# Hybrid retention, state-space and attention step: retention scores placed between two halves of the key-value products, masks ahead of the recurrence, and the last state-space outputs inside z's first unit

## The chip, the cores and the metric

One core of a Trainium2 chip runs the whole program. The metric is the device time of one execution in microseconds (us). Engine names are those of the profile: PE is TensorE, PEld its weight loads, DVE VectorE, ACT ScalarE, POOL GpSimd, SP SyncE, whose queue carries most DMAs.

## The reference, cut to what matters

Two layers of a diffusion backbone run for 128 context tokens and 512 latent tokens that share their weights: 640 token columns in 5 chunks of 128. Layer 0 mixes with retention (8 heads) and a Mamba-2 state-space recurrence (16 heads) side by side, both in both directions; layer 1 with softmax attention. Each is followed by a convolutional feed-forward block. Every recurrence is computed by chunks:

```python
def step(s, inp):
    qc, kc, vc, ac = inp
    cum = jnp.cumsum(ac, axis=1)
    ...
    scores = jnp.einsum('bigd,bjgd->bgij', qc, kc)
    y = jnp.einsum('bgij,bgrij,bjgrv->bigrv', scores, decay, vc)
    y = y + jnp.einsum('bigd,bgrdv->bigrv', qc, s) * jnp.exp(cum)[..., None]
    ...
    s = s * jnp.exp(last)[..., None] + jnp.einsum('bjgd,bjgrv,bgrj->bgrdv', kc, vc, w)
    return s, y
...
y_ret = jax.nn.silu(g) * (y_ret * gn_gain)
y_ssm = (ssm_ys[0] + ssm_ys[1]).reshape(b, L, SSM_D_INNER)
y_ssm = rms_norm(y_ssm * jax.nn.silu(z)) * norm_gain
out = jnp.concatenate([y_ret, y_ssm], axis=-1) @ w_out
...
def conv_ffn(h, w_up, conv_w, conv_b, w_down):
    u = dwconv3(h @ w_up, conv_w, conv_b)
    a, val = jnp.split(u, 2, axis=-1)
    return (jax.nn.silu(a) * val) @ w_down
```

## The kernel before, in words

Every engine has its own program, written out by hand, and semaphores tie them. No scheduler decides an order: what a function issues is what the engine runs, in that order.

**Dense stages.** A stage is a product of the 640 columns with a weight matrix, in units of 128 output features. SP loads a unit's weights into one of 4 buffers `raw`, ACT splits off a high part (`act_split`, L360), DVE the rest (`low_split`, L368), each into one of 2 buffers. PE (`pe_tile`, L379) makes for each k-tile of 128 inputs three products of the parts (high x high, low x high, high x low), in two halves of 320 columns: 6 matmuls a tile, and 8 or 7 tiles a unit. The accumulator of unit f lies in PSUM banks 0 and 1 or 2 and 3 by turns (`pj`), and must have been read (`pj_read`) before unit f + 2 begins. So unit r + 2 needs its `w_lo`, which needs PE to be done with unit r, and the reading of unit r.

**State-space part** (`pe_ssd`, `act_ssd`, `dve_ssd`, `pool_ssd`). 16 heads in 8 pairs. For pair p PE makes five decay products (`pe_decay` 0 to 4, L1250 to L1257), after the second of them the states from the keys and the weighted inputs `xw` (`pe_states`, L1281), later the products of the states with the queries (`pe_inter`, L1294). POOL makes `xw` for both directions (L1424) for pair p once the states of pair p - 2 are there. ACT turns each decay product into `E` (`act_decay`, L1268), fills `Tx` with the skip term (`act_skip`, L1340), copies the final state out (L1358) and reads the outputs (L1363). DVE runs the recurrence `Sst` (L1394, L1401), weighs `E` by the scores (L1384, L1386), scales the state outputs into `inter` (L1406) and adds them to `Tx` (L1414). The outputs of pair p (`pe_out`, L1305 and L1308, 5 chunks in two groups) need both, and PE issues them inside pair p + 1. After the last pair a ninth pass issues the outputs of pair 7 alone. Then follows stage z (`pe_z`), whose unit 0 uses banks 2 and 3, whose unit 1 needs a `w_lo` that ACT and DVE make only after ACT has read the outputs of pair 7.

**Retention** (`pe_ret`, `act_ret`, `dve_ret`). 8 heads in 4 pairs; the two heads of a pair lie in partitions 0 to 63 and 64 to 127. For pair p PE makes the scores (`pe_ret_scores`, L1611), for each chunk head 0 and head 1 in turn, into the PSUM regions `R` that also hold the outputs of pair p - 1, so it waits until ACT has copied them (`ret_yc`, L1709). DVE masks them into `PTr` (L1763). The key-value products (`pe_ret_states`, L1625, 16 calls) feed the recurrence on DVE (`recur`, L1753, six steps `ret_rec`). The outputs (`pe_ret_out`, L1644 and L1655) go through chunks 0 to 4, and wait after chunk 0 for all six steps. ACT and DVE then normalise (L1769, L1776, L1717, L1725), PE transposes (`pe_ret_turn`, L1634), DVE and ACT gate and split for stage wo_ret (`pe_wo_ret`).

**Down projections.** `pe_first` (L407) begins a stage while its input is still being made: it runs the tiles of unit 0 as they come, and inserts two tiles of unit 1 before the last tile of unit 0. In layer 0, DVE also computes parts of the modulation (`dve_late`, L563 to L576) between the steps of these stages. The stages are dn00 (8 tiles a unit), dn01 and dn02 (7 tiles).

## Time and profile before

| | |
|---|---|
| median of 3 runs | 1973.29 us (1973.1 to 1974.2) |
| the profiled execution | 1970.14 us, of which 1968.4 us from its first to its last instruction |
| PE busy | 1896.4 us, 96% of the span |
| DVE, ACT, POOL busy | 64%, 42%, 6% |
| end of the state-space part, start of z | about 258 to 266 us |
| retention pairs | about 560 to 610 us |
| starts of dn00, dn01, dn02 | about 795, 954 and 1102 us |

In a timeline, each row gives the start, the time from the start of the first instruction merged into it to the end of the last, the engine, line, operation and names, the count and, in brackets, how long the engine sat idle before it and what released it. The matmuls of PE overlap: the step from one row's start to the next start tells more than a duration. One f32 product of the program shows as two instructions of L1611, L1625, L1634, L1644, L1655 or L1281. The buffers `E` of even pairs lie in `u_sb` and `t_sb`, `Tx` lies in `hf`, `qd` in `t_sb`.

### The profile page before, as it was taken

The numbers are of one execution on the slowest core, as the hardware profiler recorded it, in microseconds if no ns is written. First come the engines' busy times: TensorE is split into PE (matmuls) and PEld (weight loads), VectorE is DVE, ScalarE is ACT, GpSimd is POOL, SyncE is SP. The second block draws the span as 40 slices with busy tenths as digits, with TensorE's granted clock in tenths as the row PEclk, the third lists the DMA queues.
The fourth block names the chain that finished last, engine by engine and source line by source line (L and its number), as shares of the span: only waits on it lengthen the run. The fifth ranks groups of instructions, "written<-read, shape, count | busy, mean of one in ns | idle before, by whom it ended". The sixth has DMA issues, their size and how long they took to land.

```text
span 1968.4 us, 33247 instructions
## 1 busy us (share of the span) xinstructions
PE 1896.4 (96%) x13415; PEld 1800.2 (91%) x13415; DVE 1267.4 (64%) x2101; ACT 817.2 (42%) x1367; POOL 122.5 (6%) x106
## 2 busy tenths in 40 slices
PE   7999999999999999999999999899999999999999
PEld 4998789999988899999999989866698999999999
DVE  5555944666877877878978876656536553553553
ACT  4645732222435355234234344555525541441441
POOL 0011200000010000000000025411100000000000
PEclk9999999999999999999999999999999999999999
DMA  8221012444321323443433322100012222222222
GB/s 308 86 77 34 17 49 89 140 147 151 102 81 54 129 100 119 144 128 115 152 128 115 110 89 68 57 1 1 1 54 61 74 69 80 76 71 76 75 69 79
DMA packets 57065, 175.96 MB, mean 89 GB/s; under 512 B 7552, under 2 KB 9472, under 8 KB 56832
## 3 DMA queue, kind: packets, MB, share of 16 engines
q1 hardware_dynamic: 55152, 172.17, 27.1%
q10 hardware_dynamic: 1808, 2.36, 0.3%
q8 instruction: 69, 1.13, 0.2%
q14 instruction: 36, 0.29, 0.0%
HBM read 170.05 MB, written 4.46 MB: 89 GB/s over the span
## 4 chain that ended last, share of the span: by engine, by line
PE 84%; DVE 9%; ACT 4%; issue 2%; DMA 1%; SPq 1%; POOL 0%; ACTq 0%; DVEq 0%
PE ps L379 70%; PE ps L2103 2%; PE ps L2088 2%; DVE t_sb L772 1%; DVE h_lo L782 1%; PE ps L879 1%; DVE w_lo L368 1%; PE ps L2056 1%; DVE PT L2220 1%; PE ps L1294 1%; PE ps L2055 1%; ACT w_hi L360 1%; PE ps L1281 1%; PE ps L1305 1%; DMA x<-in_x 1%
## 5 line engine op out<-in xcount | busy, mean ns | idle before, releaser
L379 PE MATMUL ps<-h_hi,w_hi 128*128 128x320 f32 x2768 | 637.5, 311 | 7.8 <-DVE w_lo L368 2.9
L379 PE MATMUL ps<-h_lo,w_hi 128*128 128x320 f32 x2768 | 633.0, 310 | 9.0 <-DVE h_lo L782 7.8
L379 PE MATMUL ps<-h_hi,w_lo 128*128 128x320 f32 x2768 | 629.8, 308 | 0.0
L368 DVE TENSOR_TENSOR w_lo<-raw,w_hi 128x1024 fp32r<-128x1024 f32 (+1 forms) x218 | 267.2, 1226 | 452.6 <-ACT w_hi L360 452.3
L360 ACT ACTIVATE w_hi<-raw 128x1024 fp32r<-128x1024 f32 (+1 forms) x221 | 230.6, 1043 | 695.4 <-PE ps L379 695.2
L379 PEld LDWEIGHTS ps<-h_lo,w_hi 128*128 128x128 f32 x2768 | 461.4, 188 | 16.1 <-DVE h_lo L782 14.5
L379 PEld LDWEIGHTS ps<-h_hi,w_hi 128*128 128x128 f32 x2768 | 460.5, 188 | 15.1 <-issue 5.2
L379 PEld LDWEIGHTS ps<-h_hi,w_lo 128*128 128x128 f32 x2768 | 462.6, 188 | 0.0
L379 PE MATMUL ps<-hid_hi,w_hi 128*128 128x320 f32 x704 | 160.9, 309 | 4.4 <-DVE hid_lo L981 2.5
L379 PE MATMUL ps<-hid_hi,w_lo 128*128 128x320 f32 x704 | 160.2, 308 | 0.0
L379 PE MATMUL ps<-hid_lo,w_hi 128*128 128x320 f32 x704 | 160.2, 308 | 0.0
L379 PEld LDWEIGHTS ps<-hid_hi,w_hi 128*128 128x128 f32 x704 | 117.3, 188 | 6.1 <-DVE hid_lo L981 3.8
L379 PEld LDWEIGHTS ps<-hid_lo,w_hi 128*128 128x128 f32 x704 | 117.7, 188 | 0.0
L379 PEld LDWEIGHTS ps<-hid_hi,w_lo 128*128 128x128 f32 x704 | 117.6, 188 | 0.0
L566 DVE SCALAR_TENSOR_TENSOR maccB<-mrawB,csil,maccB 128x512 f32<-128x512 f32 x168 | 115.2, 744 | 0.0
L894 DVE SCALAR_TENSOR_TENSOR x<-ps,modT,x 128x128 f32<-128x128 f32 (+2 forms) x216 | 81.2, 431 | 14.0 <-PE ps L379 14.0
L2075 DVE TENSOR_REDUCE nmax<-ps 128x1 f32<-128x640 f32 (+1 forms) x80 | 57.0, 714 | 39.4 <-PE ps L2056 39.3
L965 ACT ACTIVATE hid_hi<-hf 128x640 f32 (+1 forms) x44 | 32.5, 739 | 112.2 <-DVE hf L979 112.2
L845 ACT ACTIVATE t_sb<-ps,fconv 128x640 f32<-128x640 f32 x88 | 77.3, 879 | 0.0
L862 DVE SCALAR_TENSOR_TENSOR t_sb<-u_sb,fconv,t_sb 128x635 f32<-128x635 f32 x88 | 76.9, 874 | 0.0
L859 DVE SCALAR_TENSOR_TENSOR t_sb<-u_sb,fconv,t_sb 128x635 f32<-128x635 f32 x88 | 76.9, 873 | 0.0
L844 ACT ACTIVATE u_sb<-ps 128x640 f32<-128x640 f32 x104 | 71.4, 687 | 2.2 <-PE ps L379 2.2
(285 smaller groups left out, 2014.7 us busy)
## 6 DMA issues: line engine op xcount, KB each, us to landing
raw<-in_ffn_up SPq DMA_DIRECT2D x88, 512.0 KB, 3.6
raw<-in_hyb_in SPq DMA_DIRECT2D x49, 512.0 KB, 3.8
mrawB<-in_w_modB SPq DMA_DIRECT2D x48, 512.0 KB, 4.2
mrawA<-in_w_modB SPq DMA_DIRECT2D x64, 256.0 KB, 2.8
raw<-in_ffn_down SPq DMA_DIRECT2D x32, 448.0 KB, 3.3
raw<-in_hyb_out SPq DMA_DIRECT2D x16, 512.0 KB, 4.2
raw<-in_ffn_down SPq DMA_DIRECT2D x16, 512.0 KB, 3.6
modw<-in_w_modA SPq DMA_DIRECT2D x12, 512.0 KB, 13.3
```

The source lines that it names most:

```text
L360: act.activation(w_hi[:, i % 2, 0:n], raw[:, b % RAW, 0:n], ACT.Copy).then_inc(S("w_hi"), 1)
L368: eng.tensor_tensor(w_lo[:, i % 2, 0:n], raw[:, b % RAW, 0:n], w_hi[:, i % 2, 0:n].bitcast(F32), SUB).then_inc(S("w_lo"), 1)
L379: last = pe.matmul(pj(f)[:, hh, :], w[:, i % 2, k * 128:(k + 1) * 128], v[:, k, hh * HALF:(hh + 1) * HALF], start=(k == 0 and n == 0), sto ...
L566: ins = dve.scalar_tensor_tensor(acc, w, c, acc, MUL, ADD)
L844: act.activation(two(u_sb[:, r % 2, :]), pj(s.f0 + r), ACT.Copy).then_inc(S("cv_u"), 1)
L845: act.activation(two(t_sb[:, r % 2, :]), pj(s.f0 + r), ACT.Identity, bias=cw[:, r + 4 * j, 3:4] if isinstance(j, int) else cw[:, ds(r + 4 ...
L859: dve.scalar_tensor_tensor(t[:, :, 1:128], u[:, :, 0:127], w(0), t[:, :, 1:128], MUL, ADD).then_inc(S("cv_mid"), 1)
L862: dve.scalar_tensor_tensor(t[:, :, 0:127], u[:, :, 1:128], w(2), t[:, :, 0:127], MUL, ADD).then_inc(S("cv_done"), 1)
L894: ins = dve.scalar_tensor_tensor(xs_, out[:, hh, a0:a1], gate(r, g), xs_, MUL, ADD)
L2075: dve.tensor_reduce(nmax[:, n % 4:n % 4 + 1], score(n), AX.X, MAX, negate=True).then_inc(S("at_m"), 1)
L2088: last = pe.transpose(TP[:, b, :], Pr[n % 3][:, b * 128:(b + 1) * 128], ident)
L2103: last = pe.matmul((B6, B7)[u % 2][64 * par:64 * par + 64, 0:256].rearrange("p (m t) -> p m t", m=2), v, PT[:, u % 2, b - b0, par:AR:2, :] ...
```

## The change

Five edits, each in the program of one or two engines:

1. `pe_z`: PE issues five tiles of z's unit 0 before the outputs of pair 7, and three after. The ninth pass issues nothing on PE.
2. `act_ssd`: the skip term is made after the copy of the final state, no longer after the second decay. `pool_ssd`: of the forward direction, the product for the last chunk, which nobody reads, is left out (4 chunks in place of 5).
3. Retention on PE: of the key-value products of the next pair the first 8 calls, then the scores of head 0 (as soon as its outputs are copied), those of head 1, then the other 8 calls. Retention on DVE: the two masks come ahead of the recurrence.
4. `pe_ret_out`: chunks in the order 0, 2, 3, 1, 4; chunks 2 and 3 wait for four steps of the recurrence, 1 and 4 for six.
5. `pe_first`: in dn00, dn01 and dn02 four tiles of unit 1 come before the last tile of unit 0, in place of two.

```diff
@@ pe_first
-                steps = [(0, k) for k in range(K - 1)] + [(1, 0), (1, 1), (0, K - 1)] + [(1, k) for k in range(2, K)]
+                m = 4 if units[0][0].name[:3] == "dn0" else 2
+                steps = [(0, k) for k in range(K - 1)] + [(1, k) for k in range(m)] + [(0, K - 1)] + [(1, k) for k in range(m, K)]
@@ pe_ssd
-                if p:
+                if 0 < p < PAIRS:
                     pe_out(pe, p - 1, (0, 1, 2))
...
-                if p:
+                if 0 < p < PAIRS:
                     pe_out(pe, p - 1, (3, 4))
@@ act_ssd
                         act_decay(act, p, i)
-                        if i == 1:
-                            act_skip(act, p)
...
                                    ACT.Copy).then_inc(S("ssd_so"), 1)
+                    act_skip(act, p)
                     act_decay(act, p, 3)
@@ pool_ssd
                 for d in range(2):
-                    scaled(xw[:, p % 2, d, :, :], wdt[:, :, d, 2 * p:2 * p + 2].unsqueeze(3).to_broadcast([128, NCH, 2, 64]))
+                    n = NCH - 1 + d
+                    scaled(xw[:, p % 2, d, 0:n, :], wdt[:, 0:n, d, 2 * p:2 * p + 2].unsqueeze(3).to_broadcast([128, n, 2, 64]), n)
@@ pe_z
-            for r in range(8):
-                pe_unit(pe, stages["z"], r, 0, H)
+            s = stages["z"]
+            pe_begin(pe, s, 0)
+            for k in range(KT):
+                if k == 5:
+                    pe_out(pe, PAIRS - 1, (0, 1, 2))
+                    pe_out(pe, PAIRS - 1, (3, 4))
+                last = pe_tile(pe, s, 0, k, s.u0, s.f0, H)
+            last.then_inc(S("pe_unit"), 1)
+            for r in range(1, 8):
+                pe_unit(pe, s, r, 0, H)
@@ pe_ret_out
-            for c in range(NCH):
+            for c in (0, 2, 3, 1, 4):
...
                 if c == 0:
-                    pe.wait_ge(S("ret_rec"), 6 * p + 6)
                     pe.wait_ge(S("ret_q"), p + 1)
...
+                pe.wait_ge(S("ret_rec"), 6 * p + (6 if c in (1, 4) else 4))
@@ pe_ret
                 if p < 3:
-                    pe_ret_states(pe, p + 1)
+                    pe_ret_states(pe, p + 1, range(0, 4))
+                    for e in range(2):
+                        pe.wait_ge(S("ret_yc"), 2 * p + e + 1)
+                        pe_ret_scores(pe, p + 1, (e,))
+                    pe_ret_states(pe, p + 1, range(4, 8))
                     if p:
                         pe_ret_turn(pe, 2 * p - 1)
-                    pe.wait_ge(S("ret_yc"), 2 * p + 2)
-                    pe_ret_scores(pe, p + 1, (0, 1))
@@ dve_ret
                 if p < 3:
-                    recur(p + 1)
                     mask(p + 1, 0)
                     mask(p + 1, 1)
+                    recur(p + 1)
```

What PE issues at the end of the state-space part, before (`Sst` and `s` are the states, `E` the weighed decays, `hf` the array `Tx`, `xsy` the inputs; semaphores waited for stand in brackets):

```order
L1294 MATMUL ps<-s_58,bcT 128x128
L1305 MATMUL ps<-E_62,xsy 64x128 [waits tp_read,ssd_t,ssd_pt]
L1305 MATMUL ps<-E_63,xsy 64x128
L1308 MATMUL ps<-cst,hf 64x128 x2
L1305 MATMUL ps<-E_62,xsy 64x128
L1305 MATMUL ps<-E_63,xsy 64x128
```

and with the change (the rows of L379 go on in the same way for five tiles in all):

```order
L379 MATMUL ps<-h_hi,w_hi 128x320 [waits w_lo,ssd_so,pj_read1,ssd_rec,ssd_E]
L379 MATMUL ps<-h_hi,w_hi 128x320
L379 MATMUL ps<-h_hi,w_lo 128x320 x2
L379 MATMUL ps<-h_lo,w_hi 128x320 x2
L379 MATMUL ps<-h_hi,w_hi 128x320 x2
L379 MATMUL ps<-h_hi,w_lo 128x320 x2
L379 MATMUL ps<-h_lo,w_hi 128x320 x2
```

The wait for `ssd_t` and `ssd_pt`, which DVE raises when pair 7 is weighed and added up, now stands after thirty matmuls of z.

What PE issues between the outputs of pair 0 and those of pair 1 of the retention, before (`kw` are the weighted keys, `PTr` the masked scores):

```order
L1625 MATMUL ps<-vTM,kw 64x128 [waits ret_so,ret_rec,ret_kw]
L1625 MATMUL ps<-vTM,kw 64x128 x15
L1611 MATMUL ps<-qkT 128x128 [waits ret_yc]
L1611 MATMUL ps<-qkT 128x128 x9
L1644 MATMUL ps<-vTM,PTr 128x128 [waits ret_pt] x2
L1644 MATMUL ps<-vTM,PTr 128x128 [waits ld_s0r,ret_q,ret_rec]
```

and with the change, where the same calls have other line numbers:

```order
L1636 MATMUL ps<-vTM,kw 64x128 [waits ret_so,ret_rec,ret_kw]
L1636 MATMUL ps<-vTM,kw 64x128 x7
L1620 MATMUL ps<-qkT 128x128 [waits ret_yc]
L1620 MATMUL ps<-qkT 128x128 x4
L1620 MATMUL ps<-qkT 128x128 [waits ret_yc]
L1620 MATMUL ps<-qkT 128x128 x4
L1636 MATMUL ps<-vTM,kw 64x128 x8
L1656 MATMUL ps<-vTM,PTr 128x128 [waits ret_pt] x2
L1656 MATMUL ps<-vTM,PTr 128x128 [waits ld_s0r,ret_q]
```

The ten score calls, which went head 0, head 1, head 0 and so on, now stand as five of head 0 and five of head 1, and half of the key-value products lies behind them.

## Rows read from the trace of the kernel before

**Rows 1.** The page, busy time of PE: us, share of the span, instructions.
```profile
PE 1896.4 (96%) x13415; PEld 1800.2 (91%) x13415; DVE 1267.4 (64%) x2101; ACT 817.2 (42%) x1367; POOL 122.5 (6%) x106
```
**Rows 2.** Waits of PE: us in total, times, longest us.
```profile
PE ps L1305 <- issue: 9.0, 6, 3.8
...
PE ps L1644 <- DVE PTr L1763: 4.3, 7, 1.2
...
PE ps L379 <- DVE hid_lo L981: 2.5, 1, 2.5
```
**Rows 3.** Timeline of PE from the end of pair 7 to z.
```profile
257.68 0.39 PE L1294 MATMUL ps<-s,bcT 128*128 128x128 f32 x2
261.87 0.70 PE L1305 MATMUL ps<-E,xsy 128*64 128x128 f32 x4 [3.80 <-issue]
...
265.70 0.56 PE L379 MATMUL ps<-h_hi,w_hi 128*128 128x320 f32 x2
```
**Rows 4.** Timeline of PE, outputs of pair 5, chunks 0 to 2, and what follows.
```profile
242.93 0.44 PE L1305 MATMUL ps<-E,xsy 128*64 128x128 f32 x4 [0.43 <-issue]
...
244.39 0.50 PE L1250 MATMUL ps<-neg_r,ident_r 128*128 128x512 f32 x1
```
**Rows 5.** Timeline of DVE around the start of z.
```profile
260.29 1.48 DVE L1414 TENSOR_TENSOR hf<-hf,inter 128x512 f32<-128x512 f32 x2
...
267.49 1.23 DVE L368 TENSOR_TENSOR w_lo<-raw,w_hi 128x1024 fp32r<-128x1024 f32 x1 [5.72 <-ACT w_hi L360]
```
**Rows 6.** Timeline of DVE and POOL in pair 3.
```profile
220.13 2.48 DVE L1414 TENSOR_TENSOR hf<-hf,inter 128x512 f32<-128x512 f32 x2
...
220.80 2.93 POOL L1424 TENSOR_TENSOR xw<-xsy,wdt 128x640 f32<-128x640 f32 x2 [7.67 <-PE ps L1281]
```
**Rows 7.** A stretch: us, PE, PEld, DVE, ACT, POOL busy (instructions), granted clock, DMA share, GB/s.
```profile
568.80:572.10 3.30, 3.30 (x18) 2.63 (x18) 0.00 (x0) 0.00 (x0) 0.00 (x0) 0.50 0.00 0
```
**Rows 8.** Timeline of PE in the retention, pairs 0 and 1; products of pair 3.
```profile
559.87 1.38 PE L1611 MATMUL ps<-qkT 64*128 64x128 f32 x10
...
567.39 0.71 PE L1644 MATMUL ps<-vTM,PTr 128*128 128x128 f32 x4 [1.06 <-DVE Sr L1753]
568.03 0.49 PE L1655 MATMUL ps<-hf,t_sb 64*128 64x128 f32 x4
...
575.93 1.39 PE L1611 MATMUL ps<-qkT 64*128 64x128 f32 x20
578.48 0.49 PE L1644 MATMUL ps<-vTM,PTr 128*128 128x128 f32 x2 [1.16 <-DVE PTr L1763]
...
596.96 1.97 PE L1625 MATMUL ps<-vTM,kw 128*64 128x128 f32 x32
```
**Rows 9.** Timeline of ACT: its copies of the outputs of pairs 1, 2 and 3.
```profile
585.49 1.27 ACT L1709 ACTIVATE yv<-ps 128x640 f32<-128x640 f32 x2
...
597.80 1.26 ACT L1709 ACTIVATE yv<-ps 128x640 f32<-128x640 f32 x2
...
609.54 0.68 ACT L1709 ACTIVATE yv<-ps 128x640 f32<-128x640 f32 x1
```
**Rows 10.** Timeline of DVE in pair 3: recurrence, and statistics of head 1.
```profile
599.50 0.59 DVE L1753 SCALAR_TENSOR_TENSOR Sr<-hf,rtot,ps 128x128 f32<-128x128 f32 x2
...
602.50 1.05 DVE L1769 BATCH_NORM_STATS2 bst<-yv 128x6 f32<-128x128 f32 x5
```
**Rows 11.** Timeline of PE at dn01, last tile of unit 0 and first of unit 2.
```profile
959.73 0.56 PE L379 MATMUL ps<-hid_hi,w_hi 128*128 128x320 f32 x2 [2.50 <-DVE hid_lo L981]
...
965.12 0.45 PE L379 MATMUL ps<-hid_hi,w_hi 128*128 128x320 f32 x2
```
**Rows 12.** Timeline of DVE: reading of unit 0 at dn00, then at dn01.
```profile
806.54 1.13 DVE L894 SCALAR_TENSOR_TENSOR x<-ps,modT,x 128x128 f32<-128x128 f32 x3
...
963.05 1.13 DVE L894 SCALAR_TENSOR_TENSOR x<-ps,modT,x 128x128 f32<-128x128 f32 x3
```
**Rows 13.** Timeline of PE at dn00, first tile of unit 2.
```profile
809.24 0.46 PE L379 MATMUL ps<-hid_hi,w_hi 128*128 128x320 f32 x2
```

More of the change, by code:

```diff
@@ L1421, in pool_ssd, with scaled @@
                 xh = xs_chunks(p).rearrange("p c (h v) -> p c h v", h=2)
-                def scaled(out, by):
-                    pool.tensor_tensor(out.rearrange("p c (h v) -> p c h v", h=2), xh, by, MUL).then_inc(S("ssd_v"), 1)
+                def scaled(out, by, n):
+                    pool.tensor_tensor(out.rearrange("p c (h v) -> p c h v", h=2), xh[:, 0:n, :, :], by, MUL).then_inc(S("ssd_v"), 1)
                 if p >= 2:
@@ L1614, in pe_ret_scores, with pe_ret_states @@
                         last.then_inc(S("ret_s"), 1)
-        def pe_ret_states(pe, p):
-            pe.wait_ge(S("ret_kw"), p + 1)
-            if p:
-                pe.wait_ge(S("ret_rec"), 6 * p)
-                pe.wait_ge(S("ret_so"), p)
-            for n, (d, c) in enumerate(KV):
+        def pe_ret_states(pe, p, slots=range(8)):
+            if slots[0] == 0:
+                pe.wait_ge(S("ret_kw"), p + 1)
+                if p:
+                    pe.wait_ge(S("ret_rec"), 6 * p)
+                    pe.wait_ge(S("ret_so"), p)
+            for n in slots:
+                d, c = KV[n]
                 for e in range(2):
@@ L1626, in pe_ret_states @@
                                      start=True, stop=True)
-            last.then_inc(S("ret_kv"), 1)
+            if slots[-1] == 7:
+                last.then_inc(S("ret_kv"), 1)
         def pe_ret_turn(pe, h):
```

## The prediction

> **What bounds the kernel.** I read the page first: PE is busy 96% of the span [rows 1], so time can only be won where PE waits, where it runs at the low clock, or where it works less than its full rate. The changed kernel issues every PE instruction of the old one, so everything turns on the first two. The list of PE's waits says which places matter [rows 2]: 9.0 us before the state-space outputs of line 1305, of which 3.8 us in one place, 4.3 us before retention outputs that wait for masked scores, and a single wait of 2.5 us for the last part of a down projection's input. The timelines around these three places gave the rest.
>
> A baseline for the numbers: the profiled execution took 1970.14 us, 1.7 us over its span, and 3.15 us less than the median of the runs, 1973.29 us. I work out a difference in the profiled execution and take it off the median. A difference under 0.2%, 3.9 us, counts as none.
>
> **Part 1, the last outputs inside z.** After pair 7, PE has nothing to do from about 258.3 us until DVE has finished the sum into `Tx`; then it makes the outputs, 261.87 to 265.70, and begins z [rows 3]. Those 3.83 us are slow: ten groups of four matmuls, where in pair 5 six groups and the step to the next product took 244.39 - 242.93 = 1.46 us [rows 4], so about 0.23 us a group and 2.3 us for ten. Now z's unit 0 can begin at 258.3. A tile of it costs 0.88 us (965.12 less 959.73 us for a tile with its restart and five more gives 0.90 [rows 11]; I take 0.88). Five tiles last to 262.7, after DVE's end at 260.29 + 1.48 = 261.8 [rows 5]: no wait is left. The outputs at the full clock end at 265.0, three tiles at 267.7. What is late next is unit 1: its `w_lo` waits for ACT to read the outputs and to split, and for DVE to subtract. Before, that took from 265.70 to 267.49 + 1.23 = 268.7 [rows 3, 5], 3.0 us; now it ends at 268.0, and with a restart PE begins unit 1 at 268.2. Before it began it at 265.70 + 7.04 = 272.7. **Gain 4.5 us.** The stages that follow are paced by PE, which should keep it.
>
> The row behind the slow outputs is one of clock: a stretch of the retention shows 0.50 granted, 1.2 of 2.4 GHz, after waits of PE [rows 7, 8], and here the outputs ran at half their rate after the wait of 3.8 us. The Trainium skill, page TensorE: Matmul & The Clock Gate, section HAM oscillation, says that gaps in the stream of matmuls send the clock back to half rate and that the ramp is paid again at each. [...]
>
> **Part 2, the pair loop.** `Tx` gets its last addition while POOL works: two additions took 2.48 us in pair 3, where pair 7, without POOL, shows 1.48 us [rows 5, 6]. DVE stood still until POOL's first product was done. POOL's two products take 2.93 us, the wait of 0.4 us between them included, so 1.27 us each [rows 6]; the first falls from 640 to 512 columns, by 0.25 us, and with it the stall. It is on the path (PE's outputs wait for that sum) in pairs 2, 3 and 4: 0.75 us. The later skip term frees the third decay 0.9 us sooner in pair 0, where PE waits for ACT, but in pairs 1 and 2 it stands before the fourth decay and gives back about 0.25 us each. Bounds of this second effect are a gain of 0.9 us and a loss of 0.5; I take a gain of 0.25. **Gain 1.0 us**, between 0 and 1.7.
>
> **Part 3, retention.** Three terms.
>
> (a) The order of chunks. In pair 0 the four matmuls of chunk 1 waited for all six steps of the recurrence, and the state products began at 568.03 [rows 8]. With chunk 2 first, its own matmuls (0.64 us) run during the wait, and two steps less of 0.3 us are waited for [rows 10]: 1.2 us. The wait of 1.06 us [rows 8], the longest just before the slow stretch 568.8 to 572.1 [rows 7], goes with it, and I therefore expect that stretch to run at the full clock: 3.3 us at half rate gave back 1.5 us. Gain 2.7 us, 1.2 if the clock falls all the same.
>
> (b) Scores by one head. Five calls of one head alone took 1.38 us, ten calls of two heads in turn 1.39 us [rows 8]. So two heads in turn run beside each other, and in the new order, five of head 0 and then five of head 1, they don't: 2.6 us in place of 1.3, in each of pairs 1, 2 and 3. Against it stands the wait for masks, 1.16 us before the first outputs of pair 1 and 0.24 us for head 1 [rows 8, 2], which the products put behind the scores now cover. PE comes out even if nothing else holds it.
>
> (c) Something else does. ACT can copy the outputs of a pair only when it has normalised the pair before. This chain is: copy of head 0; 0.7 us until PE may overwrite it; 2.6 us of scores; 0.95 us for the second half of the products (1.97 us for all [rows 8]); 0.2 us to DVE; the recurrence, now behind the masks and so behind these products, 1.5 us, and the statistics of head 1, which began 3.0 us after it, half of that being masks [rows 10]; from there 7.04 us to the next copy, 602.50 to 609.54 [rows 9, 10]. Sum: 0.7 + 2.6 + 0.95 + 0.2 + 1.5 + 7.04 = 13.0 us a pair. Before, two pairs took 609.54 - 585.49 = 24.05 us [rows 9]. Now they take 26.0: a loss of 2.0 us. For the first such round I have no row: with (a) without its clock, the copy of pair 1 comes 0.1 us sooner than before, because the first round loses about 1.1 us to the same chain. So the last copy, for which stage wo_ret waits, comes 0.1 us (first round), 1.5 us (clock) sooner and 2.0 us later. **Loss 0.4 us.** Its bounds: a gain of 3 us if heads overlap more than the rows say, a loss of 2 if the clock doesn't stay up. I take the sum, since both prices under it were read in this place.
>
> **Part 4, down projections.** At dn01 PE waited 2.50 us for the last input and began that tile at 959.73 [rows 11]. Two more tiles of unit 1 now fill 1.76 us of the wait. But unit 2 must wait until DVE has read unit 0, which it did at 963.05 + 1.13 = 964.2 [rows 12], a time set by the same late input. Unit 2 begins at 964.4, before at 965.12 [rows 11]: a gain of 0.7 us only. At dn00 there was no wait; now unit 0 ends 1.76 us later, DVE reads it until 806.54 + 1.13 + 1.76 = 809.4 [rows 12], and PE wants unit 2 at 809.24 [rows 13]: with the step to PE and a restart 0.4 us, and some 0.2 us more at unit 3, as DVE has its modulation work queued behind the reading. At dn02 DVE is late with unit 2 already, so neither. **Gain 0.1 us**, between a loss of 0.6 and a gain of 1.8.
>
> **Sum.** 4.5 + 1.0 - 0.4 + 0.1 = 5.2 us. 1973.3 - 5.2 gives 1968.1 us.
>
> **Rivals.**
> *The clock falls once more in the retention.* New waits stand there, some 1.3 us before a pair's scores and 2.3 before wo_ret, and the scores of one head keep half the array idle. For it: the slow stretch of pair 0 came after a wait of only 1.06 us [rows 7, 8]. Against: 2.50 us at dn01 left the clock up. A fall costs 1.5 us; one or two give 1969.6 to 1971.1 us. Chance 0.23. [...]
> *POOL gets in first.* If its first product starts before the first addition into `Tx` rather than at the second, DVE stands still at both and the sum is 1 us or more late in a pair. POOL started 0.67 us after the additions began [rows 6], and both keep their distance from the outputs, so it is unlikely but in pair 0 or 1. Price 1 to 2 us: 1969.6. Chance 0.10.
> *Scores of one head cost less*, because head 1 starts under head 0 or the products fill in. Then the waits for masks are won, up to 1.2 us in three pairs, and the chain shortens: 1965.0. Against it are two rows that show 1.38 us for five calls. Chance 0.10.
> *Slower.* The retention is held at the low clock in every pair. Its place is the four pairs; it decides once four falls of 1.5 us are reached, more than the 5.2 us won; with six the time is 1977 us. For it: PE's work is thin there in each pair. Against: pair 1 had waits of 1.16 and 0.24 us [rows 8, 2] and no slow stretch after them. Chance 0.04.
> *The wait stays where it was*, if z's unit 0 can't begin at 258.3 for a semaphore I misread: its list holds the decays, the recurrence and the state copy of pair 7, all done by then. Gain of part 1 down to 0, 1972.6. Chance 0.03.
>
> **Numbers.** The forecast itself, with its small terms, has 0.50: about 1966.8 to 1969.6. Adding the rivals on both sides until 2 in 10 are left out gives 1965.6 to 1971.0. Faster than 1969.4: most of the forecast (0.46), part of the clock (0.05) and POOL (0.04) cases, the cheap scores (0.10): 0.65. Slower by over 3.9 us, the one case: 0.04. The rest, 0.31, is within.
>
> **What would show it.** Right: no wait of PE between pair 7 and z; outputs of pair 7 in 2.3 us between tiles of z, followed by a wait under 0.7 us before unit 1; two rows of scores of 1.3 us in each pair; copies of outputs 13.0 us apart; full clock in pair 0; at dn01 a wait of 0.7 us before the last tile and a new one of about 1 us before unit 2; at dn00 a new wait of 0.3 us. Wrong: copies 11.7 us apart or less (then the head-by-head price was not real), or a low clock in the retention.

## The result, and the profile after

| | before | changed |
|---|---|---|
| median of the runs, us | 1973.74 (1973.1 to 1974.83, 4 runs) | 1962.03 (1960.37 to 1965.63, 4 runs) |
| ratio to before, 95% interval | | 0.994 [0.9925, 0.9955] |
| the profiled execution, us (its span) | 1970.14 (1968.4) | 1965.63 (1963.8) |

11.7 us are gained where 5.2 were forecast, and 1962.0 lies under the range of 1965.6 to 1971.0. The two profiled executions alone differ by 4.5 us, which looks like the forecast. But they are single draws: other executions of the same two kernels differ by 13.8 us, and that is the lesson of this case.

The page of the changed kernel, busy time, which answers to [rows 1]:
```profile
PE 1899.8 (97%) x13415; PEld 1803.0 (92%) x13415; DVE 1267.7 (65%) x2101; ACT 818.5 (42%) x1367; POOL 119.6 (6%) x106
```
Its waits of PE, which answer to [rows 2]; columns as there:
```profile
PE ps L379 <- DVE x L895: 4.8, 4, 2.1
PE ps L1306 <- issue: 4.5, 5, 1.2
...
PE ps L379 <- ACT yv L1723: 2.4, 1, 2.4
```
The 9.0 us ahead of the state-space outputs are 4.5, and the single wait of 3.8 us is gone. So are the masks' waits of pairs 1 to 3, which made up most of the 4.3 us. New are waits of PE on ACT's copies, the longest ahead of wo_ret. Timeline of PE from pair 7 into z's unit 1, for [rows 3]:
```profile
255.89 0.39 PE L1295 MATMUL ps<-s,bcT 128*128 128x128 f32 x2
256.03 0.54 PE L379 MATMUL ps<-h_hi,w_hi 128*128 128x320 f32 x2
...
260.60 0.44 PE L1306 MATMUL ps<-E,xsy 128*64 128x128 f32 x4
...
262.94 0.55 PE L379 MATMUL ps<-h_hi,w_hi 128*128 128x320 f32 x2
...
266.02 0.56 PE L379 MATMUL ps<-h_hi,w_hi 128*128 128x320 f32 x2 [0.18 <-DVE w_lo L368]
```
z begins without a wait; the outputs take 262.94 - 260.60 = 2.34 us, and unit 1 waits 0.18 us. The copies of ACT, pairs 0 to 3, for [rows 9]:
```profile
564.76 1.30 ACT L1723 ACTIVATE yv<-ps 128x640 f32<-128x640 f32 x2 [6.32 <-PE ps L1667]
576.89 1.27 ACT L1723 ACTIVATE yv<-ps 128x640 f32<-128x640 f32 x2
589.46 1.27 ACT L1723 ACTIVATE yv<-ps 128x640 f32<-128x640 f32 x2
602.03 1.27 ACT L1723 ACTIVATE yv<-ps 128x640 f32<-128x640 f32 x2
```
The last two are 12.57 us apart, before 12.0 in the mean. PE at the first tile of wo_ret:
```profile
602.76 0.90 PE L379 MATMUL ps<-h_hi,w_hi 128*128 128x320 f32 x2 [2.37 <-ACT yv L1723]
```
PE at dn01, for [rows 11]:
```profile
955.51 0.56 PE L379 MATMUL ps<-hid_hi,w_hi 128*128 128x320 f32 x2 [0.73 <-DVE hid_lo L982]
...
960.02 0.56 PE L379 MATMUL ps<-hid_hi,w_hi 128*128 128x320 f32 x2 [0.73 <-DVE x L895]
```
At dn00 PE's weight loads wait twice for DVE's reading, 0.6 us in all:
```profile
PEld ps L379 <- DVE x L895: 0.6, 2, 0.3
```
Last, the slow stretches: times in which the granted clock is 0.50, that is 1.2 GHz of 2.4. Windows of the changed kernel, columns as in [rows 7]:
```profile
14.70:21.60 6.90, 5.86 (x13) 0.73 (x14) 4.52 (x6) 4.52 (x7) 0.00 (x0) 0.51 1.04 396
182.00:185.40 3.40, 3.40 (x14) 3.17 (x15) 2.17 (x4) 3.17 (x11) 0.00 (x0) 0.50 0.01 2
601.80:608.70 6.90, 5.94 (x23) 5.90 (x24) 4.12 (x26) 2.43 (x5) 0.00 (x0) 0.51 0.19 76
1110.40:1113.80 3.40, 3.40 (x14) 3.40 (x14) 3.40 (x8) 1.26 (x2) 0.00 (x0) 0.50 0.45 148
1274.30:1277.70 3.40, 3.40 (x17) 2.42 (x13) 0.60 (x2) 1.48 (x3) 0.05 (x1) 0.50 0.00 0
```
The kernel before had its own: of 3.4 us at 15.8, 183.1, 261.6 and 568.8, and of 6.8 us at 1275.3 us. (The first window and the third of the changed kernel are 6.8 us long as well.)

### The profile page after: what moved, and what is told of

Read it like the earlier page. It is cut to its first block, busy times and chain, and to the rows that moved or that the text cites. A ratio compares the mean times of both kernels' runs of the same rounds, so it can differ in the third digit from the quotient of the medians.

```text
span 1963.8 us, 33247 instructions
## 1 busy us (share of the span) xinstructions
PE 1899.8 (97%) x13415; PEld 1803.0 (92%) x13415; DVE 1267.7 (65%) x2101; ACT 818.5 (42%) x1367; POOL 119.6 (6%) x106
## 4 chain that ended last, share of the span: by engine, by line
PE 83%; DVE 9%; ACT 4%; issue 2%; DMA 1%; POOL 1%; SPq 0%; ACTq 0%; DVEq 0%; POOLq 0%
PE ps L379 69%; PE ps L2117 2%; PE ps L2102 2%; DVE t_sb L773 1%; DVE w_lo L368 1%; DVE h_lo L783 1%; ACT w_hi L360 1%; PE ps L880 1%; PE ps L1295 1%; DVE PT L2234 1%; PE ps L2070 1%; PE ps L2069 1%; DVE x L895 1%; PE ps L1282 1%; DMA modw<-in_w_modA 1%
## 5 line engine op out<-in xcount | busy, mean ns | idle before, releaser
L379 PE MATMUL ps<-h_hi,w_hi 128*128 128x320 f32 x2768 | 638.6, 312 | 9.0 <-DVE w_lo L368 3.2
L379 PE MATMUL ps<-h_lo,w_hi 128*128 128x320 f32 x2768 | 633.7, 310 | 9.4 <-DVE h_lo L783 8.2
L379 PE MATMUL ps<-h_hi,w_lo 128*128 128x320 f32 x2768 | 630.8, 309 | 0.0
L379 PEld LDWEIGHTS ps<-h_lo,w_hi 128*128 128x128 f32 x2768 | 462.2, 188 | 16.5 <-DVE h_lo L783 14.9
L379 PEld LDWEIGHTS ps<-h_hi,w_hi 128*128 128x128 f32 x2768 | 461.1, 188 | 16.7 <-issue 5.2
L379 PEld LDWEIGHTS ps<-h_hi,w_lo 128*128 128x128 f32 x2768 | 463.4, 188 | 0.0
L379 PE MATMUL ps<-hid_hi,w_hi 128*128 128x320 f32 x704 | 161.7, 311 | 3.8 <-DVE x L895 2.8
L379 PE MATMUL ps<-hid_hi,w_lo 128*128 128x320 f32 x704 | 160.8, 309 | 0.0
L379 PE MATMUL ps<-hid_lo,w_hi 128*128 128x320 f32 x704 | 160.7, 309 | 0.0
L379 PEld LDWEIGHTS ps<-hid_hi,w_hi 128*128 128x128 f32 x704 | 117.8, 188 | 5.9 <-issue 2.6
L379 PEld LDWEIGHTS ps<-hid_hi,w_lo 128*128 128x128 f32 x704 | 118.3, 188 | 0.0
L379 PEld LDWEIGHTS ps<-hid_lo,w_hi 128*128 128x128 f32 x704 | 118.2, 188 | 0.0
```

The costliest lines, as they stand in the source:

```text
L379: last = pe.matmul(pj(f)[:, hh, :], w[:, i % 2, k * 128:(k + 1) * 128], v[:, k, hh * HALF:(hh + 1) * HALF], start=(k == 0 and n == 0), sto ...
```

## The experiments

Every kernel was timed beside the kernel before, on the same chip; the chip changed between groups of experiments. A stretch is counted below as one where it is 3.4 us long, as two where 6.8 and as three where 10.2.

**The same kernels again.** No edit.

> The kernel before, unchanged, for a second trace and a spread of its runs. Theory A (the schedule explains it): the profiled execution of before (1970.1 us) was as good as any, and the 3.2 us between it and the median are nothing of the program's; the second trace then shows the same slow-clock stretches, at about 183, 262 and 569 us, and a sum of PE's waits within 0.5 us. Theory B (the clock explains the rest): executions of the same program differ in how many stretches at 1.2 GHz they have, at about 1.5 us each; the new trace shows another number or other places, and its time follows the count: near 1973.5 us with about two stretches more than the first trace had.

> The changed kernel, unchanged. Its first trace (1965.6 us) had three stretches at the low clock after the start that cost time (at 182, 602 to 609 and 1110 us), and its other runs took 1960.4 to 1962.1. Theory B: a trace without the long stretch at wo_ret shows about 1961 to 1962 us, with the same waits of PE to 0.3 us. Theory A: the waits themselves differ between executions.

before_again: 1973.9 us, ratio 1.0005 [0.9996, 1.0013]. after_again: 1961.44, 0.9948 [0.9935, 0.996]. Their profiled executions took 1973.93 and 1960.09 us (spans 1972.1 and 1958.3), the first at its median and the second 1.35 us better than its own; the spans differ by 13.8 us. Timeline of PE, first decay and first output of the pair loop, first state product of the retention, first tiles of dn00, dn01, dn02 and of layer 1's first down projection. before_again:
```profile
174.15 0.50 PE L1250 MATMUL ps<-neg_r,ident_r 128*128 128x512 f32 x1 [0.46 <-ACT t_sb L845]
192.28 0.32 PE L1305 MATMUL ps<-u_sb,xsy 128*64 128x128 f32 x1
561.93 0.66 PE L1625 MATMUL ps<-vTM,kw 128*64 128x128 f32 x8
798.65 0.45 PE L379 MATMUL ps<-hid_hi,w_hi 128*128 128x320 f32 x2
953.53 0.46 PE L379 MATMUL ps<-hid_hi,w_hi 128*128 128x320 f32 x2
1105.66 0.46 PE L379 MATMUL ps<-hid_hi,w_hi 128*128 128x320 f32 x2
1615.45 0.45 PE L379 MATMUL ps<-hid_hi,w_hi 128*128 128x320 f32 x2
```
after_again:
```profile
175.24 0.50 PE L1251 MATMUL ps<-neg_r,ident_r 128*128 128x512 f32 x1 [0.46 <-ACT t_sb L846]
190.95 0.32 PE L1306 MATMUL ps<-u_sb,xsy 128*64 128x128 f32 x1
554.93 0.66 PE L1636 MATMUL ps<-vTM,kw 128*64 128x128 f32 x8
788.13 0.45 PE L379 MATMUL ps<-hid_hi,w_hi 128*128 128x320 f32 x2
943.61 0.46 PE L379 MATMUL ps<-hid_hi,w_hi 128*128 128x320 f32 x2
1093.43 0.46 PE L379 MATMUL ps<-hid_hi,w_hi 128*128 128x320 f32 x2
1601.59 0.46 PE L379 MATMUL ps<-hid_hi,w_hi 128*128 128x320 f32 x2
```
The differences of neighbouring rows are a ledger of the change, for these two executions:

| stage | before_again | after_again | gain | forecast |
|---|---|---|---|---|
| pair 0, decay to output | 18.13 | 15.71 | 2.4 | 0.25 |
| pairs, z and on to the retention | 369.65 | 363.98 | 5.7 | 5.25 |
| retention, on to dn00 | 236.72 | 233.20 | 3.5 | -0.4 |
| dn00, on to dn01 | 154.88 | 155.48 | -0.6 | -0.6 |
| dn01, on to dn02 | 152.13 | 149.82 | 2.3 | 0.7 |
| dn02 and layer 1's attention | 509.79 | 508.16 | 1.6 | 0 |

The rest, -1.1 us, is the start, ahead of any edit. Where the gain exceeds the forecast, there are stretches in before_again, in pair 0 beside the shorter wait of PE on the third decay. Its windows:
```profile
181.80:188.60 6.80, 6.17 (x27) 5.93 (x28) 5.13 (x8) 3.02 (x12) 0.00 (x0) 0.50 0.00 1
263.70:267.10 3.40, 3.40 (x28) 3.07 (x24) 0.00 (x0) 1.08 (x2) 0.00 (x0) 0.51 0.00 0
567.50:577.80 10.30, 9.66 (x52) 7.86 (x54) 0.92 (x4) 0.33 (x1) 0.24 (x1) 0.50 0.00 0
963.50:966.90 3.40, 3.40 (x14) 3.40 (x14) 2.52 (x5) 0.95 (x1) 0.00 (x0) 0.50 0.17 37
1280.90:1284.30 3.40, 3.16 (x12) 1.94 (x12) 1.64 (x3) 0.96 (x4) 1.04 (x1) 0.50 0.12 39
```
And two of after_again, its one stretch behind the start, and the retention at the full clock:
```profile
182.20:185.60 3.40, 3.06 (x12) 2.69 (x12) 1.98 (x3) 3.40 (x13) 0.00 (x0) 0.50 0.01 5
555.00:612.00 57.00, 50.66 (x493) 43.78 (x494) 40.58 (x149) 32.83 (x72) 7.18 (x3) 1.00 0.03 11
```
Away from the start, which waits for DMAs, the longer waits of one kernel are the same in each of its executions, to about 0.02 us, where no stretch comes between; the stretches differ. PE's wait for ACT's third decay in pair 0, in before_again and in after_again:
```profile
182.43 0.80 PE L1250 MATMUL ps<-neg_r,ident_r 128*128 128x512 f32 x1 [1.20 <-ACT t_sb L1268]
...
182.68 0.80 PE L1251 MATMUL ps<-neg_r,ident_r 128*128 128x512 f32 x1 [0.34 <-ACT t_sb L1269]
```
In the retention the kernel before takes 233.99 us to dn00 with one stretch (its first profile) and 236.72 with three: 1.37 us each, and 232.6 with none, an estimate by that price. The changed kernel takes 233.20 with none and 235.9 with two (its first profile), 1.35 each, but only 235.1 with two in after_third below, where the wait ahead of wo_ret is 1.32 us in place of 2.37 and so takes part of the cost. The stretches behind dn01's wait and in the attention cost 1.5 and 1.6 us in before_again.

**One part alone, and all but one.** z_only keeps of the diff the edits to `pe_ssd` and `pe_z`; ret_only those of `pe_ret`, its functions and the order on DVE; loop_only those of `act_skip`'s place and of POOL's products; dn_only the new count of tiles ahead of unit 0's last:
```diff
+                m = 4 if units[0][0].name[:3] == "dn0" else 2
```
no_ret, no_loop and no_dn are the whole change without the part they name.

> Only the last state-space outputs inside z's unit 0. My prediction gave this part 4.5 us. Theory A: 4.5 to 5.0 us under before. Theory B: the same, since the gain of the full clock (1.5 us) is in it in nearly every execution of before: the wait of 3.8 us is long; 4.5 to 5.5 us under before.

> Only the retention edits (split scores, masks first, chunk order). Predicted: a loss of 0.4 us with one fall of the clock avoided. In the trace of the changed kernel the pairs came out 0.8 us better than before, up to the first tile of wo_ret. Theory A: 0.5 to 1.0 us under before. Theory B: in most executions of before the retention pairs run with two or three stretches at the low clock, so 3 to 5 us under before, and a trace shows none between 560 and 600 us.

> The kernel before with the edits of the pair loop alone: the skip term behind the state copy on ACT, and four chunks in place of five in POOL's first product. So far the whole change gains 12 us, its z part alone 4.3 and its retention part alone loses 1.7, so 9 us lie in the loop, in the down projections, or in what the parts do together. Theory A (each part wins the waits that its own lines show, and PE's low clock follows waits nearby): PE's wait in pair 0 falls from 1.20 to 0.36 us and the waits in pairs 2, 3 and 4 from 1.43 to 1.21, together 1.5 us, and with the wait in pair 0 shortened the slow stretch at 183 us is 3.4 us long and no longer 6.8, another 1.5: 1970.5. Rival B (the loop does nothing but its waits): 1972 to 1972.5. Rival C (the 9 us are the loop's): under 1966.

> The kernel before with the edit of the down projections alone: two more tiles of unit 1 ahead of unit 0's last tile in dn00, dn01, dn02. Theory A: by the waits it gains 0.7 at dn01 and gives some back at dn02, and the wait of 2.50 us at dn01 becomes two of 0.73, after which there is no slow stretch at 963 us, as there was in three of four profiles that had the long wait; one more stretch later, at 1280 us, stays: 1971 to 1972. Rival B (no connection of the clock with that wait; the stretch at 963 stays): 1972.8 to 1973.5. Rival C (the missing 9 us are here): under 1967.

> The change without its retention part: z, loop and down projections as changed. Theory A (the parts add): the z part gives 4.3, the loop 1.5 to 3, the down projections 1 to 2: 1964 to 1966.5, with a slow stretch at 568 us as before. Rival (the retention part, a loser of 1.7 us alone, wins once the others are there, since the slow stretches at 568 and 602 then go): 1968 to 1969, a slow stretch at 568 us, and 7 us to the whole change.

> The change without its pair loop part: z, retention and down projections as changed. Theory A (the parts add by their waits): 1.5 us more than the whole change, 1963, up to 1964.5 with one more slow stretch at 183 us. Rival (the loop keeps later waits short of what lowers the clock, and is needed for the gain): 1967 or more, with slow stretches at 568 or 602 us that the whole change has not.

> The change without its down projection part. Theory A (the part gains 0.77 us at dn01, loses 0.60 at dn00, and keeps the clock up behind dn01, a stretch of 1.54 us that three of four profiles with the long wait had): 1962.6 to 1963.5, the wait of 2.50 us at dn01 back, dn00 56.19 us and dn01 53.4. Rival (the stretch comes somewhere else in its place, as the run of this part alone on the kernel before looks like): 1961.4 to 1962.

| kernel | median | ratio [interval] | mean granted clock, median of the runs |
|---|---|---|---|
| before (29 runs) | 1973.46 | | 0.991 |
| z_only | 1969.16 | 0.9982 [0.9973, 0.999] | 0.993 |
| ret_only | 1975.12 | 1.0009 [0.9999, 1.0019] | 0.990 |
| loop_only | 1971.88 | 0.9991 [0.9982, 1.0] | 0.991 |
| dn_only | 1974.51 | 1.0011 [1.0002, 1.002] | 0.990 |
| no_ret | 1965.05 | 0.9956 [0.9942, 0.997] | 0.994 |
| no_loop | 1964.46 | 0.9959 [0.9944, 0.9973] | 0.994 |
| no_dn | 1964.95 | 0.996 [0.9946, 0.9973] | 0.994 |
| the change (after_again) | 1961.44 | 0.9948 [0.9935, 0.996] | 0.995 |

Alone the parts give 4.3, -1.7, 1.3 and -1.3 us, 2.6 in sum; together 12. Taken out of the whole, retention, loop and down projections are worth 3.6, 3.0 and 2.7 us by the medians (no_dn beside after_third's 1962.3 below). These three have five runs each and intervals that overlap that of the whole change, so single values can be off by 2 us. Each part's stage does in every profile what its lines say: from the first output to the retention 369.65 us before, 364.62 in z_only (5.0 gained, of which 1.5 is the stretch at 264), 363.96 with the loop's edit (0.66 more, POOL's shorter product); pair 0 takes 16.7 to 18.1 us in the seven profiles without the loop's edit and 15.5 to 16.0 in twelve of the thirteen with it. The exception is no_ret, 16.9 us, whose slow time there is 6.8 us long. dn00 loses 0.60 in all with its edit, and from dn01 to dn02 kernels with the dn edit take 149.8 us against 152.1 with a stretch and 150.6 without.

Two places show that an edit also takes stretches away. At the start of z, all five profiles with the old, unfilled wait of 3.8 us have one at 261 to 265 us, and none of the fourteen with z's edit has. At dn01, five of the seven profiles with the wait of 2.50 us have one behind it, and none of the thirteen with the dn edit. Over the whole run the clock column shows less: z_only rises to 0.993, the loop's part stays at 0.991, and dn_only and ret_only are at 0.990. That the medians of the parts don't add up goes with these differences; why a part brings stretches elsewhere isn't shown. With the old retention, five of the seven profiles have three stretches in a row there, beginning between 562 and 571 us, loop_only two and the first profile one. The whole change's three profiles have two, none and two, all from 590 us on. ret_only has two, at 568.2 and 602.3 us.

**The two halves of the retention part.** On no_ret: plus_order has the chunks as `for c in (0, 2, 3, 1, 4)` with the shorter wait; plus_split has the scores between the products and the masks ahead of the recurrence, chunks in the old order.

> z, pair loop and down projections as changed, and of the retention part the order of chunks alone (0, 2, 3, 1, 4, with the wait for four steps of the recurrence); scores stay two heads in turn and behind the products. The kernel without it takes 1965.05, the whole change 1961.4 to 1962. Theory A (the order takes the wait of 1.06 us in pair 0, and with it the three slow stretches that begin at 567 us; the scores by one head only cost): PE's wait gone, 1.2 us, and one to three slow stretches of 1.4 us less: 1960 to 1962.5, as good as the whole change or better; copies of outputs 11.5 to 12.3 us apart. Rival (the slow stretches have another cause and stay at 567): 1963.8.

> z, pair loop and down projections as changed, and of the retention part the scores between two halves of the products and the masks ahead of the recurrence; chunks of the outputs in the old order. Theory A (this half of the part costs, by scores that take 2.6 us for two heads one after the other): the wait of 1.06 us in pair 0 and slow stretches after it stay; copies of outputs 12.5 us apart or more: 1965 to 1967. Rival (this half is where the retention part wins, by the masks' waits that it covers): 1961 to 1963 and 12.0 us apart.

plus_order took 1963.92 us, 0.9948 [0.9935, 0.9962], and plus_split 1968.54, 0.997 [0.996, 0.9981]. Waits of PE in the retention; plus_order:
```profile
568.91 0.49 PE L1653 MATMUL ps<-vTM,PTr 128*128 128x128 f32 x2 [1.16 <-DVE PTr L1772]
```
and plus_split:
```profile
563.10 1.22 PE L1656 MATMUL ps<-vTM,PTr 128*128 128x128 f32 x4 [1.06 <-DVE Sr L1767]
...
578.74 0.71 PE L1656 MATMUL ps<-vTM,PTr 128*128 128x128 f32 x4 [1.10 <-DVE Sr L1767]
```
The order takes the wait of pair 0 away, 1.1 us (from the first state product to dn00 235.95 us with three stretches, no_ret 237.05 with three). The stretches come all the same, at 571.1, behind the masks' wait of 1.16. The split alone puts the recurrence behind the masks, and every pair then waits for it: 240.42 us to dn00 with four stretches. Neither half alone has what the eight profiles have that join the whole retention part to z's edit: no stretch in the retention before 590 us. Freedom from both waits isn't enough for that, since ret_only has neither and still a stretch at 568.2, behind a wait of 0.50 us that all these kernels share.

**What a wait does to the clock.** before_fill: the kernel before, with this ahead of `pe_out(pe, 7, (0, 1, 2))`:
```diff
+                    pe.wait_ge(S("ssd_E"), 5 * PAIRS)
+                    pe_keep(pe, flat[:, 832:1024], (192,) * 9)
```


> The kernel before with nine matmuls of 192 columns ahead of the outputs of pair 7, into a bank that nobody uses then and whose results nobody reads, some 2.9 of the 3.8 us that PE waits there. The result doesn't change. Theory A (the slow stretch at 262 us is the wait's doing, and costs the outputs of pair 7 their 1.5 us): outputs in 2.3 us in place of 3.83, no slow stretch between 260 and 268 us, 1971.7 to 1972.2. Rival B (the slow outputs have another cause, their own length of 64 rows and groups of four): 3.8 us again, 1973.2 to 1973.5. Rival C (the wait there decides what later stretches do as well, which would be why the z part carries so much of the whole gain): under 1970.

1973.03 us, 0.9994 [0.9985, 1.0003]. Timeline of PE, and the window:
```profile
261.72 3.09 PE L677 MATMUL ps<-cst 128*128 128x192 f32 x18
265.69 0.44 PE L1305 MATMUL ps<-E,xsy 128*64 128x128 f32 x4 [0.88 <-issue]
...
267.46 0.42 PE L1305 MATMUL ps<-E,xsy 128*64 128x128 f32 x4
```
```profile
260.00:268.00 8.00, 7.12 (x75) 6.71 (x73) 4.62 (x7) 1.28 (x5) 0.00 (x0) 1.00 0.10 33
```
The outputs take 0.44 us for two groups of four, as in pair 5 [rows 4], at the full clock. From the first output to the retention 368.10 us, 1.55 less than before_again. So theory A holds there: the wait was what the slow outputs came from. Over the run the median is 1.0 us lower, which its interval doesn't tell from nothing, and all the later stretches came (570, 966, 1215, 1283 us), so rival C falls: it is not this wait that decides the later ones.

after_fill puts the same kind of matmuls into five waits of the changed kernel.

> The changed kernel with matmuls of 192 columns that nobody reads in five of the waits that it still has: six in pair 0 ahead of its third decay (2.3 us), two and four ahead of the scores of pairs 2 and 3 (0.7 and 1.35), six ahead of wo_ret (2.4), five ahead of unit 2 of dn02 (2.05). Theory A (a wait of PE of 1 to 2.4 us is what a slow stretch follows, and a stretch costs 1.3 to 1.5 us of matmuls): no stretch at 182, 602 and 1110 us, of which a profile had one to four: 1957 to 1960, faster than the changed kernel. Rival B (filling changes nothing): 1961 to 1962. Rival C (the fill delays what follows, by PE that is busy when the semaphore comes): over 1962.5.

1962.47 us, 0.9941 [0.9928, 0.9955]: no different from the changed kernel. Its profile has no stretch behind any filled wait, and none in the attention either; but it has three at the start, which no edit touches, and began the pair loop at 176.4 us (the profiles range from 174.1 to 177.7). From decay to output pair 0 took 15.9 us without a stretch, with one 15.7 in after_again: there a single stretch costs nothing. Two in a row did cost about 1 us in no_ret.

**Can the changed kernel be bettered?** both_heads makes the scores once ACT has read both heads:
```diff
-                    for e in range(2):
-                        pe.wait_ge(S("ret_yc"), 2 * p + e + 1)
-                        pe_ret_scores(pe, p + 1, (e,))
+                    pe.wait_ge(S("ret_yc"), 2 * p + 2)
+                    pe_ret_scores(pe, p + 1, (0, 1))
```
best is both_heads with `m = 4` for dn01 only; dn01_alone has that second edit without the first; dn01_fill is dn01_alone with after_fill's matmuls but for those of pair 0.

> The changed kernel again, on the chip of the next three: 1961 to 1962.5. Theory A: between pair 0's first decay and its first output 15.7 to 16.0 us with or without slow stretches, as in both its earlier profiles; retention 59.1 us, 1.3 more for each slow stretch in it.

> The changed kernel with the scores of a pair made of both heads in turn once ACT has read both, still between the two halves of the products. Theory A (ten calls take 1.3 us in place of 2.6, and the chain from copy to copy is what bounds the retention): scores begin 0.6 us later and end 0.7 us sooner, copies of outputs 11.9 us apart in place of 12.56, the stretch from the first products to the last turn 57.2 us in place of 59.1 without slow stretches: 1959.5 to 1960.3. Rival (scores by one head cost nothing on the path, since DVE takes them one head after the other): 59 us or more and 1961.4 to 1962.5.

> both_heads, and the two more tiles only in dn01, where PE waited; dn00 and dn02 as before. Theory A: another 0.60 us at dn00: 1958.8 to 1959.8, faster than both kernels. Rival: the same as both_heads within 0.3, if what dn00 loses is made good before PE needs it.

> The changed kernel with the two more tiles of unit 1 only in dn01; dn00 and dn02 as before. Theory A (dn00 had no wait, and what the two tiles cost there is lost): dn00 takes 56.19 us in place of 56.79, wait at dn02 1.71 in place of 2.05 us with the same end, all else alike: 1961.0 to 1961.7. Rival (no_dn's 2.6 us show that the whole edit counts, through the stretches it moves): over 1963.

> dn01_alone with matmuls of 192 columns that nobody reads in the waits ahead of the scores of pairs 2 and 3 (two and four), ahead of wo_ret (six) and ahead of unit 2 of dn02 (five). Theory A (a slow stretch follows such a wait and costs 1.3 to 1.5 us): none at 590 to 609 and at 1110 us, of which profiles of the changed kernel had none to three; retention 59.1 us: 1958.5 to 1960.5. Rival (they cost too little in most executions to be seen): the same as dn01_alone within 0.5.

after_third 1962.3 us, 0.9945 [0.9932, 0.9959]; both_heads 1964.61, 0.9961 [0.9947, 0.9974]; best 1965.02, 0.9954 [0.9941, 0.9968]; dn01_alone 1962.42, 0.9943 [0.9929, 0.9957]; dn01_fill 1961.26, 0.9937 [0.9923, 0.995]. ACT's copies in both_heads:
```profile
564.34 1.30 ACT L1722 ACTIVATE yv<-ps 128x640 f32<-128x640 f32 x2 [6.32 <-PE ps L1667]
576.56 1.27 ACT L1722 ACTIVATE yv<-ps 128x640 f32<-128x640 f32 x2
589.35 1.28 ACT L1722 ACTIVATE yv<-ps 128x640 f32<-128x640 f32 x2
```
12.22 and 12.79 us apart, against 12.13 and 12.57: worse, where I expected 11.9. best, with the same retention, has 12.20 and 12.80; no stretch comes between these copies. Scores of both heads cost PE less, but they begin later, as they wait for both copies, and the masks of head 0 then wait for them all. That this is why DVE is late is my reading of the order, and no run tests it alone. The PE time of scores was not what the chain hung on; by the copies the rival was right, though its medians are too noisy to say so. dn01_alone gets its 0.60 us at dn00 back (first tile to first tile 154.88 again) and its median doesn't show it: its profile has two stretches in the attention. dn01_fill has one such stretch and, with after_again, the lowest medians of all, but its 0.9937 and dn01_alone's 0.9943 have intervals that overlap nearly whole. Nothing here is shown to beat the changed kernel.

## Why the prediction was wrong

The steps, one by one:
- **Part 1** was right, and short by half a us: 5.0 against 4.5, with unit 1 waiting 0.18 us, and the stretch at 262 was worth the 1.5 us that I had read into it (before_fill).
- **Part 2.** POOL's term was right: 0.66 against 0.75 us. The skip term was mis-sized: I gave it 0.25 us by the waits on ACT and its lines, with bounds of -0.5 and 0.9. Pair 0 takes 15.5 to 16.0 us with the edit (16.9 in no_ret) and took 16.7 to 18.1 before, 0.8 us less between the two first profiles and 2.4 between the two second ones. The earlier third decay shortens PE's wait from 1.20 to 0.34 us. Six of the seven profiles without the edit have 6.8 us of slow clock there, and eleven of the thirteen with it have 3.4, which costs nothing there.
- **Part 3**, (a): the wait goes, 1.1 us (plus_order), and I counted one stretch with it. Five of the seven profiles with the old retention have three. (b): scores of two heads one after the other take 2.08 us, not 2.6. In after_again the products follow on the scores of pair 3 at 592.74 - 590.66:
```profile
590.66 2.16 PE L1620 MATMUL ps<-qkT 64*128 64x128 f32 x20 [1.34 <-ACT yv L1723]
592.74 1.09 PE L1636 MATMUL ps<-vTM,kw 128*64 128x128 f32 x16
```
(c): the chain was long by about that half us: 12.57 us from copy to copy, forecast 13.0. But both_heads took 0.7 us off the scores and made the chain longer, so its link from the scores was not as I had it. Without any stretch the changed retention is 0.6 us slower than the old would be by the estimate above (233.2 against 232.6), where my terms without the clock lose 1.9. With three stretches before and none or two after it wins 3.5 us or 0.8 to 1.6.
- **Part 4**: 0.73 and 0.73 us of waits at dn01, 0.77 us gained, 0.60 lost at dn00 in two waits for DVE's reading, as forecast. Missed is the stretch behind dn01's long wait: I took from one execution that ran without it that the clock stays up. before_again, z_only, ret_only, loop_only and before_fill had it; before and no_dn, with the same wait, had not.
- **The step that failed** is in the baseline: "I work out a difference in the profiled execution and take it off the median." That step puts at nothing every slow stretch that the median execution has and the profiled one hasn't. The profiled execution was 3.15 us better than the median, and I said so and went on. It has six stretches, a mean clock of 0.995; the runs' median is 0.991, which at two levels of clock is 2 x 0.009 x 1972 = 35 us slow, some ten stretches. The changed kernel's runs have 0.995 in the median, 2 x 0.005 x 1960 = 20 us, six.
- **What that is worth** can be worked out in two ways, and they don't agree. Four or five stretches less at 1.4 us are 6 to 7 us, and the schedule terms as measured (3.5 for part 1 without its stretch, 0.7 and 0.8 for part 2, -0.6, 0.2) are 4.6: together about 11, against 11.7 measured. My sum had 3.0 and 2.2. But in the 86 runs of the kernel before that were timed beside the other experiments, a thousandth of mean clock goes with only 0.95 us, so that four of them are 3.8 us. And runs of the two kernels with the same clock still differ by more than 4.6 us: at 0.994 the medians are 1971.2 (8 runs) and 1965.1 (2 runs), at 0.995 they are 1970.1 (3) and 1962.2 (5). The mean clock counts stretches and doesn't say where they fall. So 4 to 7 us belong to the number of stretches, an estimate, and the rest to the schedule and to stretches that fall where they cost less. The sum of 11 is no proof of the split.

The rival "clock falls once more" came true in its place and was outweighed: in the changed kernel's first profile the clock is low from 601.8 to 608.7 us, and that stretch begins within the wait of 2.37 us ahead of wo_ret. The Trainium skill, TensorE: Matmul & The Clock Gate, HAM oscillation, tells of a kernel whose matmuls wait some 3 to 5 us for a DMA again and again, and whose clock falls each time. The trace agrees for the one wait of such a length, the 3.8 us ahead of z, filled and unfilled. For the shorter waits, 1.06 to 2.50 us, the section names no fall, and the runs show both: behind 2.50 us at dn01 a stretch in five executions and none in two. "POOL gets in first", "the wait stays" and "slower" did not happen. "Scores cost less" was half right: 2.08 us in place of 2.6, and the chain 0.4 us shorter than forecast, but not shorter than before.

**Open** stays why one execution has a stretch behind a wait and the next has not, why ret_only and dn_only win in their own stages and are no faster over the run, and why the attention, whose instructions nobody moved, has one to three stretches in 13 of the 20 profiles and none in seven, after_again, after_third and after_fill among them. All seven profiles of kernels with at most one part of the change have one there, and six of the thirteen others: something upstream matters, and no run shows what.

## What to carry to other kernels

A single profile is one draw. Before a difference is taken off a median, compare the profiled execution's time and mean clock with those of the runs: here it lacked some four of ten slow stretches. Compare stage by stage two executions whose clocks are like those of their medians, and look at more than one. Price a wait of a us or more at its length plus the chance of a stretch of low clock behind it. Judge parts of a change together as well as alone: alone, two of the four parts here showed no gain over the run. And find out which engine a chain hangs on before costing another engine's work in it: cheaper scores on PE left the copies of the retention later.

## What was not expected of the hardware

- Slow stretches at 1.2 GHz last with PE busy throughout some of them (10.20 of 10.20 us from 571.1 in plus_order). One of 3.4 us costs about 0.9 to 1.7 us in the retention, at dn01 and in the attention, and nothing in pair 0.
- The same program with the same waits has more or fewer of them from run to run. The 86 runs of the kernel before, timed beside the others, have mean clocks of 0.989 to 0.995, by the count above six to thirteen stretches, and times of 1969.2 to 1977.5 us; clock and time have a correlation of -0.88.
- Nine matmuls of 192 columns in a wait of 3.8 us kept the clock up: no stretch at 260 to 268 us, and 1.55 us won there.
- Scores with 64 rows: five calls of one head and then five of the other take 2.08 us, against 1.39 for the same ten with the heads in turn and 1.38 for five calls alone. So the second head costs 0.7 us, not its own 1.3.
